# Inverse deviations of q, k and the convolution by exp(-ln(v)/2) and one Newton step

## The reference

```python
def rms_norm(x, g):
    y = xf * lax.rsqrt(jnp.mean(xf * xf, axis=-1, keepdims=True) + EPS)   # EPS = 1e-6
    return (y * g.astype(jnp.float32)).astype(x.dtype)
...
z = jnp.einsum("bsd,dc->bsc", xn, w_in[l])          # columns B | C | h | q | k | v
y_conv = short_gated_conv(gb, gc, hh, conv_w[l], conv_b[l])
q = rms_norm(q, q_gain); k = rms_norm(k, k_gain)     # per head of 64, 8 heads
... scores over a band of 9 chunks of 64, softmax, times v
y_mix = concatenate([group_rms_norm(y_conv, ..., 64), group_rms_norm(y_attn, ..., 64)])
x = x + y_mix @ w_out
x = x + square(relu(rms_norm(x) @ w_mlp_in)) @ w_mlp_out
```

## Time and profile before

| | |
|---|---|
| three runs | 1225.32, 1231.07, 1230.14 us |
| profiled execution | 1227.32 us, of which the span of the trace is 1225.5 us |
| mean granted TensorE clock | 0.983 |
| TensorE matmuls busy | 1164.6 us |
| VectorE busy | 777.3 us |
| ScalarE busy | 529.7 us |
| GpSimd busy | 610.1 us |

### The profile page before, as it was taken

The page is one execution under the profiler, slowest core; times in us unless marked ns, Lnnn a source line. Parts: engine busy times, 40 slices in busy tenths (PEclk is TensorE's granted clock), DMA queues, the critical chain, the costliest instruction groups (busy, mean ns, idle before and its releaser), DMA issues.

```text
span 1225.5 us, 14666 instructions
## 1 busy us (share of the span) xinstructions
PE 1164.6 (95%) x5368; PEld 946.2 (77%) x5368; DVE 777.3 (63%) x867; ACT 529.7 (43%) x827; POOL 610.1 (50%) x331
## 2 busy tenths in 40 slices
PE   5999999998999998899799999999998999999998
PEld 4878877876887686688678888888876888888886
DVE  6566866785677668744534344453448787676887
ACT  5554443446344545321444544545453333343330
POOL 4211230223032203001478787877869789697892
PEclk9999988998999899999999999999999999999999
DMA  7310110111011041311135444444386534435324
GB/s 224 106 35 18 55 34 17 34 36 51 0 51 36 1 172 52 138 53 69 60 104 172 155 138 157 154 160 148 138 292 249 198 129 161 166 112 196 122 87 155
DMA packets 98512, 135.81 MB, mean 111 GB/s; under 512 B 8072, under 2 KB 52112, under 8 KB 98456
## 3 DMA queue, kind: packets, MB, share of 16 engines
q1 hardware_dynamic: 95104, 131.13, 31.5%
q10 hardware_dynamic: 3352, 3.94, 1.1%
HBM read 97.27 MB, written 39.34 MB: 111 GB/s over the span
## 4 chain that ended last, share of the span: by engine, by line
PE 83%; DVE 9%; issue 2%; DMA 2%; POOL 1%; ACT 1%; SPq 0%; DVEq 0%; ACTq 0%; POOLq 0%
PE PJ L1399 18%; PE PJ L1646 8%; PE SC L1646 8%; PE OS L1646 7%; PE PJ L1680 6%; PE PT L1680 6%; PE SC L1680 6%; PE OS L1680 6%; PE PJ L1472 5%; PE SC L1430 4%; DVE sq L954 3%; PE OS L1454 2%; PE PT L1441 2%; DVE sql L944 2%; DMA gB<-in_norm_mlp_g 1%
## 5 line engine op out<-in xcount | busy, mean ns | idle before, releaser
L1399 PE MATMUL PJ<-actT,wsl 128*128 128x512 f32 (+1 forms) x1176 | 313.5, 410 | 0.0
L1399 PEld LDWEIGHTS PJ<-actT,wsl 128*128 128x128 f32 x1176 | 214.3, 195 | 50.4 <-issue 5.7
L562 POOL TENSOR_TENSOR ring<-b,ring 128x1024 fp32r<-128x1024 f32 x48 | 137.7, 2877 | 37.8 <-ACT ring L883 37.7
L1309 DVE TENSOR_TENSOR ring<-hraw,ring 128x1024 fp32r<-128x1024 f32 x56 | 151.0, 2731 | 3.8 <-ACT ring L878 3.8
L484 POOL CAST wsl<-raw 128x1024 fp32r<-128x1024 f32 x24 | 27.0, 1127 | 240.7 <-PE PJ L1399 225.8
L878 ACT ACTIVATE ring<-hraw 128x1024 fp32r<-128x1024 f32 x56 | 59.2, 1057 | 134.4 <-PE OS L1680 63.6
L520 POOL TENSOR_TENSOR w1a<-w1r,w1a 128x512 fp32r<-128x512 f32 x32 | 50.5, 1580 | 122.0 <-ACT w1a L815 122.0
L1646 PE MATMUL OS<-actT,w1a 128*128 128x512 f32 x384 | 93.1, 391 | 2.0 <-POOL w1a L520 2.0
L664 ACT ACTIVATE prob<-prob,negm 128x640 f32<-128x640 f32 (+4 forms) x64 | 44.6, 696 | 114.3 <-DVE negm L1024 114.1
L1680 PE MATMUL PJ<-ring 128*128 128x512 f32 x336 | 82.4, 395 | 6.0 <-POOL ring L562 4.4
L1646 PEld LDWEIGHTS OS<-actT,w1a 128*128 128x128 f32 x384 | 72.3, 189 | 17.3 <-POOL w1a L520 2.2
(11 more groups left out here) (182 smaller groups left out, 2224.9 us busy)
## 6 DMA issues: line engine op xcount, KB each, us to landing
hraw<-hidd SPq DMA_DIRECT2D x56, 512.0 KB, 3.6
w1r<-in_w_mlp_in SPq DMA_DIRECT2D x16, 1024.0 KB, 6.1
b<-in_w_mlp_out SPq DMA_DIRECT2D x16, 1024.0 KB, 6.4
hidd<-hs SPq DMA_DIRECT2D x64, 256.0 KB, 2.0
raw<-in_w_in SPq DMA_DIRECT2D x24, 512.0 KB, 3.6
hidd<-h SPq DMA_DIRECT2D x48, 256.0 KB, 2.2
xin<-in_x SPq DMA_DIRECT2D x8, 512.0 KB, 8.5
woraw<-in_w_out SPq DMA_DIRECT2D x8, 512.0 KB, 7.4
```

Source lines behind the costliest of these rows:

```text
L562: nc.gpsimd.tensor_tensor(duo(n)[1][LO], W2_SRC[name][:, 2 * d:2 * d + 2], duo(n)[1][HI].bitcast(F32), ALU.subtract).then_inc(s["wl2_done" ...
L1309: vec.tensor_tensor(duo(n)[0][LO], hraw[:, n % HRING], duo(n)[0][HI].bitcast(F32), ALU.subtract).then_inc(s["hl2_done"], 1)
L1399: last = mm(PJ[:, g % 2, cols], wsl[:, w % NSLOT, a, k], actT[:, b, k, c], start=(r == 0), stop=(r == 3 * KD - 1))
```

## The change

`deviation` now runs three steps on ScalarE: Ln of sum/64 + eps into `sq`, Exp of -0.5 times that in place (a first inverse deviation r0), and Square of r0 times sqrt(0.5/64) into the new tile `rt` (so rt = r0² / 128). `inverse` on VectorE becomes two scalar_tensor_tensor: w = (SS + 64 eps) * rt, which now is the reader that frees `SS`, and r = (w - 1.5) * r0, the Newton step with its sign turned. For the convolution `CG` is negated once. The sign cancels in the product of q and k. `rt` lies on the bytes of `sql`, so GpSimd waits for the end of `inverse(it - 1, 5)` before it writes `sql` of norm 1. `o_dev` becomes Ln and Exp, and `o_norm` has three small scalar_tensor_tensor where there was one reciprocal. The square roots of the input norm and of the MLP's norm stay.

```diff
@@ ScalarE
             def deviation(it, n):
                 act.wait_ge(s["ones_done"], it * 6 + (n + 1))
-                act.activation(sq[:, zbuf(n)], SS[:, :], ACT.Sqrt, bias=eps[:, 0:1], scale=1.0 / HD).then_inc(s["ss_read"], 1)
+                act.activation(sq[:, zbuf(n)], SS[:, :], ACT.Ln, bias=eps[:, 0:1], scale=1.0 / HD).then_inc(s["dev_done"], 1)
+                act.wait_ge(s["dev_done"], it * 18 + 3 * n + 1)
+                act.activation(sq[:, zbuf(n)], sq[:, zbuf(n)], ACT.Exp, scale=-0.5).then_inc(s["dev_done"], 1)
+                act.wait_ge(s["dev_done"], it * 18 + 3 * n + 2)
+                act.activation(rt[:, n % 2], sq[:, zbuf(n)], ACT.Square, scale=(0.5 / HD) ** 0.5
+                               ).then_inc(s["dev_done"], 1)
...
             def o_dev(it, g):
                 act.wait_ge(s["oss_done"], it * 2 + (g + 1))
-                act.activation(osd[:, :], oss[:, :], ACT.Sqrt, bias=eps[:, 0:1], scale=1.0 / HD).then_inc(s["osd_done"], 1)
+                act.activation(osd[:, :], oss[:, :], ACT.Ln, bias=eps[:, 0:1], scale=1.0 / HD).then_inc(s["osd_done"], 1)
+                act.wait_ge(s["osd_done"], it * 4 + (2 * g + 1))
+                act.activation(osd[:, :], osd[:, :], ACT.Exp, scale=-0.5).then_inc(s["osd_done"], 1)
@@ VectorE
             def inverse(it, n, part=None, extra=0):
-                b = zbuf(n)
-                c = slice(0, HALF) if part is None else slice(part * (HALF // 2), (part + 1) * (HALF // 2))
+                r0, w = sq[:, zbuf(n)], rt[:, n % 2]
                 if part != 1:
+                    dve.wait_ge(s["dev_done"], it * 18 + 3 * n + 3)
+                    vec.scalar_tensor_tensor(w, SS[:, :], HD * EPS, w, ALU.add, ALU.mult).then_inc(s["ss_read"], 1)
+                if part != 0:
                     dve.wait_ge(s["ss_read"], it * 8 + (TURN[n] + 3 + extra))
-                op = vec.reciprocal(sq[:, b, c], sq[:, b, c])
-                if part != 0:
-                    op.then_inc(s["rs_done" if n < 4 else "rsc_done"], 1)
+                    vec.scalar_tensor_tensor(r0, w, 1.5, r0, ALU.subtract, ALU.mult).then_inc(s["rs_done" if n < 4 else "rsc_done"], 1)
...
             def o_norm(it, g):
-                dve.wait_ge(s["osd_done"], it * 2 + (g + 1))
-                vec.reciprocal(ors[:, :], osd[:, :]).then_inc(s["ors_done"], 1)
-                dve.wait_ge(s["ors_done"], it * 2 + (g + 1))
+                dve.wait_ge(s["osd_done"], it * 4 + (2 * g + 2))
+                vec.scalar_tensor_tensor(ors[:, :], oss[:, :], HD * EPS, osd[:, :], ALU.add, ALU.mult).then_inc(s["ors_done"], 1)
+                dve.wait_ge(s["ors_done"], it * 6 + (3 * g + 1))
+                vec.scalar_tensor_tensor(ors[:, :], ors[:, :], -0.5 / HD, osd[:, :], ALU.mult, ALU.mult).then_inc(s["ors_done"], 1)
+                dve.wait_ge(s["ors_done"], it * 6 + (3 * g + 2))
+                vec.scalar_tensor_tensor(ors[:, :], ors[:, :], 1.5, osd[:, :], ALU.add, ALU.mult).then_inc(s["ors_done"], 1)
+                dve.wait_ge(s["ors_done"], it * 6 + (3 * g + 3))
...
@@ GpSimd, ahead of sql of norm 1
+                        pool.wait_ge(s["rsc_done"], it * 2 + 1)
@@ VectorE, once, ahead of the loop
+            vec.tensor_scalar(prm_all[:, CG, :], prm_all[:, CG, :], -1.0, None, ALU.mult).then_inc(s["prm_g"], 1)
```

More of the change, by code:

```diff
@@ L130, in build @@
         sqh = put("sqh", [P, 2, HALF], F32R)
+        rt = nc.alloc_sbuf_tensor_at("rt", [P, 2, HALF], F32, offset=top[0])
         sql = put("sql", [P, 2, HALF], F32R)
@@ L197, in build @@
         sm_done ptlo_done rl_done osc_done osq_done oss_done ors_done on_done
-        zs_done sq_done sqh_done hi_done vcopy_done cs_done vhi_done exp_done pthi_done ss_read osd_done
+        zs_done dev_done sq_done sqh_done hi_done vcopy_done cs_done vhi_done exp_done pthi_done ss_read osd_done
         wohi_done wo_ready woq_ready ymhi_done ym_ready mix_done hadd_done wlast_done
@@ L907, in _ @@
             vec = nc.vector
+            dve.sem_inc(s["rsc_done"], 1)
             vec.memset(eps[:, :], EPS).then_inc(s["masks_ok"], 1)
@@ L1005, in conv_scale @@
             def conv_scale(it, n):
-                dve.wait_ge(s["rsc_done"], it * 2 + (n + 1))
+                dve.wait_ge(s["rsc_done"], it * 2 + (n + 2))
                 vec.scalar_tensor_tensor(ymix[:, 4 * n:4 * n + 4, bass.ds(it, 1), :].rearrange("p t o c -> p t (o c)"),
@@ L1200, in _ @@
             dve.wait_ge(s["prm_g"], 1)
+            vec.tensor_scalar(prm_all[:, CG, :], prm_all[:, CG, :], -1.0, None, ALU.mult).then_inc(s["prm_g"], 1)
+            dve.wait_ge(s["prm_g"], 2)
             inverse(0, 0, 0, extra=1)
-            inverse(0, 0, 1)
+            inverse(0, 0, 1, extra=1)
             qk_scale(0, 0)
```

## The result

The changed kernel takes 1237.84 us (median of 7 runs, 1236.91 to 1243.41), the kernel before, run beside it, 1227.69 us (7 runs, 1225.32 to 1231.07): ratio 1.0084, 95% interval 1.0065 to 1.0104. So the change makes the kernel slower by 10 us. The forecast was 1224 us; the rival *two sets* had said 1245. The profiled execution took 1239.75 us, with a span of 1238.0 us at a mean granted clock of 0.981.

A forecast was written before the change was run, and what follows sets the result against it. TensorE was taken as the bound (busy 95% of the span, 83% of the chain), VectorE mattering only where TensorE waits for it. Seams -2.4, end -1.5, start +1.0 make -2.9 from 1227.32, so 1224 us; range 1212 to 1248.

The forecast's parts named there:

- two sets: Rival, chance 0.33: Ln and Exp load different tables, two loads per deviation and `o_dev`; slower, 1245 us.
- Tables: ScalarE, between Ln and Exp: no load taken, at scarcely better than even; bounds nothing and one load of 1.283 us.
- that case: The forecast's own case, no load between Ln and Exp: 1224 us, range 1219 to 1230, chance 0.42.
- The fourth unit: Norm 3's squares, where TensorE waits 2.18 us for L944: GpSimd's L486 holds VectorE, not the reciprocal; gain 0, four times.
- The seam: Between iterations: 0.40 us (probabilities) plus 0.4 (end of L486), 0.8 us per seam, 2.4 over three; bounds 0 and 3.2 per seam.
- margin of 0.15 us: At the seam: GpSimd's L486 starts ahead of the `prm` copy by 0.15 us, so the copy ends with L486.
- one long wait: Rival, chance 0.10: seam waits become one of about 2 us, the clock falls, two more seams pay 3.4 us; 1231 us.
- The eleventh unit: Term of the two sets rival: `o_dev` and norm 4 make four loads for two, +0.9 us, four times, 3.6.
- The start: Ahead of the loop: ScalarE's `deviation(0, 0)` 1.3 us longer, 0.2 to 0.3 slack; +1.0 us, bounds 0 and 1.3.
- The end: `inverse(it, 5)` falls from 3.34 to 1.5 us, but `o_transpose` waits 2 us for `SS`; gain about 1.5, bounds 0 and 1.8.
- The steps themselves: Dependent ScalarE step 0.633 + 0.03 us, new VectorE pair 2 times 0.75; 46 us of VectorE's 777.3 saved over 24 norms.

The follow-up runs named there:

- e1: The changed kernel with the one table set that holds both Ln and Exp loaded ahead of the loop; 1220.95 us, ratio 0.9948.
- e4: The kernel before with norm 3's subtraction `squares_lo(3)` put ahead of `qk_scale(2)`, reciprocals kept; 1214.32 us, ratio 0.9912.
- e9: The kernel before (square root and reciprocal) with `squares_lo(3)` ahead of `qk_scale(2)` and the `prm` copy not waiting for `o_store`; 1211.04 us, ratio 0.9855.
- e7: The changed kernel with one table set, `squares_lo(3)` ahead of `qk_scale(2)` and the `prm` copy not waiting for `o_store`; 1195.73 us, ratio 0.9732.
- e5: The changed kernel with one table set and the `prm` copy not waiting for `o_store`; 1210.61 us, ratio 0.9849.
- e12: The changed kernel with its 64 loads, the `prm` copy not waiting for `o_store`; 1231.09 us, ratio 1.0011.

## Why the prediction was wrong, step by step

**The step that failed is the term *Tables*.** I took no load between Ln and Exp "at scarcely better than even" and put its two ends, 0 and 1.283 us each, into two cases instead. The trace has the upper end at every one of the 32 places. With the lower end, e1, the time is 1220.95 us against 1224 forecast for that case, inside its own range of 1219 to 1230. The Trainium skill (ScalarE: Activation LUTs, Table sets) says that ln followed by exp takes one load from a set that has both. The change's trace disagrees, with 64 loads; with that set loaded by hand e1 has it as the page says, 3 loads. The sentence of the Trainium skill (ScalarE activation tables: per-element evaluation and per-set limits, Table sets in the compiler and the runtime) on the longest run, which I had weighed against the rival, isn't borne out either: in the change no Ln shares a load with the Exp behind it. Which program placed the loads no trace shows. The margin between the two cases was thin (0.42 against 0.33) and the decision hung on no row; the better answer to such a tie is to say which line of the kernel would settle it, and here that is the one line of e1.

**The fourth unit, 0 gain: right.** L487 runs from 192.28 to 194.96 and L955 from 192.67 to 195.52, 0.56 us behind it, as in the earlier trace rows:

```profile
192.28 2.68 POOL L487 TENSOR_TENSOR wsl<-raw,wsl 128x1024 fp32r<-128x1024 f32 x1
192.67 2.85 DVE L955 TENSOR_TENSOR sql<-sq,sqh 128x512 fp32r<-128x512 f32 x1
...
195.65 0.49 PE L1431 MATMUL OS<-sqh,ones 128*128 128x512 f32 x1 [2.35 <-DVE sql L955]
```

The wait even grew by 0.17 us, to 2.35, since TensorE was there a little sooner: the product with V in front of it took 0.40 us (at 191.06) against 0.51 before. e4 shows the mechanism by its removal. What I hadn't seen is that this held only while GpSimd did: with the order swapped the reciprocal is the next thing that TensorE waits for, and the same saving is worth 2.2 us per iteration there (e9 against e7).

**The seam, 0.8 us each: the waits named did go, the copy went both ways.** In e1 the waits for the probabilities and for `o_transpose` are gone as worked out, and the three seams are 0.2, 0.6 and 2.6 us shorter than before, 3.5 where the sum had 2.4. The total is near by luck: the two seams where GpSimd was first gave less than the 0.8 taken, and the third, where the copy went ahead, gave the most. The margin of 0.15 us between GpSimd and the copy was sized well: it fell on either side. Two seams of the changed kernel (first and third), GpSimd's L487 beside the copy L1169:

```profile
170.79 2.35 POOL L487 TENSOR_TENSOR wsl<-raw,wsl 128x1024 fp32r<-128x1024 f32 x1
170.89 2.28 DVE L1169 COPY prm<-prm_all 128x6 f32 x1 [0.56 <-ACT ymix L689]
...
173.44 0.90 PE L1449 MATMUL SC<-kT,qT 64*128 64x128 f32 x3 [1.90 <-DVE negm L1037]
...
406.73 2.42 POOL L487 TENSOR_TENSOR wsl<-raw,wsl 128x1024 fp32r<-128x1024 f32 x1
406.73 0.17 DVE L1169 COPY prm<-prm_all 128x6 f32<-128x6 f32 x1 [0.48 <-ACT ymix L689]
```

0.10 us behind GpSimd it takes 2.28 us, at the same stamp 0.17. The Trainium skill (GPSIMD Engine Reference, Specifications) has the SBUF interfaces of GpSimd shared with VectorE, with contention for VectorE instructions in a 2-port mode or with two SBUF inputs. The rows agree as far as they go: the copy ends at 173.17, GpSimd's subtraction at 173.14; in what mode a copy with one input runs they don't show. e5 and e12, which move the copy, get the wait back. That a lost race costs 1.90 us and the clock can fall behind it was in *one long wait*: the race was lost at two seams of three, in e1 and in the change, with a granted clock of 0.61 to 0.63 behind it at both of the change's and at one of e1's.

***Two sets*: the mechanism was right and its sum 7 us too high.** At the seam it had 3 us, three times 9. The loads cost 3.64 us there (33.75 us at seam 3 of the change, 30.11 in e1, neither with a lost race), and the rest of the change, the shorter queue of VectorE and the copy that here goes ahead of GpSimd, gives 2.62 back (32.73 before against 30.11). The difference is +1.0, which is what seam 3 shows; seams 1 and 2 add the lost race and the clock, +3.4 and +6.0, and together that makes 10.4 where 9 and part of 2 to 3 for the clock were expected. Within the seam I had missed one term: `SS` is freed by VectorE behind ScalarE's three steps, 1.60 us of TensorE at norm 0. I had seen this wait at the end, but not here. The eleventh unit (3.6) was wrong as four times 0.9: it is 0 in three iterations, and in the last one the stretch from norm 2 to norm 5 is 2.5 us longer than in e1, 0.7 of it a longer wait for `on` (1.99 against 1.32) and about 1.7 a granted clock of 0.949 between norm 4 and norm 5, where e1 has 1.00. The start was 4.5 instead of 3 and the end 0 instead of +0.5.

**The start, +1.0.** In e1 it is 1.5 in the length to norm 2, 1.24 of it the wait for GpSimd's `sql`: just beyond the upper bound of 1.3. GpSimd's subtraction started 1.0 us later, as worked out, but also took 1.81 us in place of 1.30 (at 42.79): VectorE's `qk_scale` of norm 0 now comes early enough to start 0.06 us ahead of it, at 42.73, where a reciprocal ran beside it before. I hadn't counted that.

**The end, -1.5.** In e1 it is -1.9; in the change 0, since the loads of norm 5 and `o_dev` stand ahead of the next output weights on ScalarE, and TensorE's wait for GpSimd's part of these weights was 2.50 us against 1.56 in e1. The new wait of `o_transpose` on `SS` was 0.58 us in e1, not 2, because TensorE got there 1.3 us later, counted from norm 5.

**The steps themselves** were sized right: 631 ns for a dependent one on ScalarE (0.633 taken), 690 and 762 ns for the new pair (0.75 taken for each). VectorE's total fell by 39.6 us, not 46: the lines alone give 82.4 - 18.3 - 16.6 = 47.5, the small steps of `o_norm` take 2.4 back, and the other 5.5 lie in other steps and in how far neighbouring records overlap. The sum also had GpSimd idle in the places of the new steps, and that is not so everywhere: in the change L969 takes 1.68 us at 50.58, beside a subtraction of GpSimd (L496, at 50.42, 1.29 long), and in e1 the first small step of `o_norm` takes 2.37 us at 486.90.

## What to carry to other kernels

When a change adds a function to ScalarE, count the table loads in front of it first; if two functions alternate and no row shows them side by side, load by hand the set that has both, or treat the pair of loads as the likely case. Loads are free where ScalarE has slack (24 of the 64 here) and cost time where the next unit's inputs queue behind them (3.6 us a seam), so price them by place and not by number. And an engine that is off the path because something else holds its place is not off it for good: alone the saving was worth 6.5 us (e1), behind the swap and the split 15.3.

## What the runs showed of the hardware

- A load of a table takes 1.283 us and the next ACTIVATE starts 0.01 us behind it (146.47, 1.28 long, then 147.76). The load in turn starts 0.02 us behind the ACTIVATE in front of it (147.76, 0.69 long, then 148.47). The Trainium skill (ScalarE: Activation LUTs, What ACT_TABLE_LOAD costs) adds about 1.38 us of draining per switch; these rows leave no room for it, and the measurement decides.
- A copy of 128x6 on VectorE takes 0.16 us by itself and 2.28 us when it starts 0.10 us after a subtraction of 128x1024 on GpSimd. It works the other way too: GpSimd's subtraction of 128x512 takes 1.30 us beside a reciprocal of VectorE (41.81 in the kernel before) and 1.74 to 1.82 us when VectorE's `qk_scale` of 128x512 has started 0.06 to 0.14 us ahead of it (42.79 in e1, 43.88 and 157.88 in the change).
- The clock does not follow a wait of a given length with certainty: behind 2.34 us of waiting in the same place it was granted at 0.62 over 9 us in one kernel and at 1.00 in another. A fall costs about 3.1 us (42.97 against 39.91 us for the same products). What decides whether it falls is not shown. Executions of one kernel differ in it too: those of e1 took 1216.46 to 1223.28 us at mean granted clocks of 0.987 to 0.982. So a difference of some us between two kernels with such waits can be the clock's and not the change's.
